# Where the conditioning slabs stand in the stream of weight slabs: behind every two or three weight slabs instead of behind each slab of a body's second half

## The reference

```
mods = silu(c) @ w_ada + b_ada                  # 9 vectors of 2048: shift, scale, gate of three stages
h = modulate(rms(x), sh1, sc1);  x += 0.5 * g1 * (silu(h@Wa) * (h@Wb)) @ w_ffn1_out
h = modulate(rms(x), sh2, sc2);  P = h @ w_in -> z, xBC, dt, u, gate_a, gate_b
A = ssd(conv(xBC), dt, z) @ w_a_proj;   B = glu(gelu(s5(u)) @ w_b_glu)
x += g2 * ((sigmoid(gate_a)*A + sigmoid(gate_b)*B) @ w_out)
h = modulate(rms(x), sh3, sc3);  x += 0.5 * g3 * swiglu(h, w_ffn2_in) @ w_ffn2_out;  rms(x)
```

## Time and profile before

| | |
|---|---|
| three runs | 2624.9 us median (2623.9 to 2632.23) |
| the profiled execution | 2625.14 us, span 2623.3 us |
| granted TensorE clock, mean over the span | 0.957 |
| busy share of the span | PE 94%, DVE 69%, ACT 39%, POOL 10% |

### The profile page before, as it was taken

How to read it: one execution, slowest core, us unless ns; L and a number is a source line. 1 busy time by engine, 2 the same in 40 slices (tenths; PEclk the granted TensorE clock), 3 DMA queues, 4 the chain that set the end, 5 groups by cost and what they waited for, 6 DMA issues and landing times. The chain is left out here.

```text
span 2623.3 us, 40243 instructions
## 1 busy us (share of the span) xinstructions
PE 2462.9 (94%) x16344; PEld 2272.9 (87%) x16344; DVE 1799.5 (69%) x2107; ACT 1015.1 (39%) x1074; POOL 271.7 (10%) x284
## 2 busy tenths in 40 slices
PE   6689999999999999899899979989999999999998
PEld 5668789978889988788799979989888899888998
DVE  4677877787786658899867776756876655444544
ACT  1043343334343344334434443333433444434433
POOL 0028823131421000000000000000000000000000
PEclk6599999999999989999999989999999999999999
DMA  8866786778787655454556656756687756555553
GB/s 293 319 225 241 266 294 241 272 276 309 260 310 247 234 181 193 146 179 159 176 178 208 209 177 225 242 200 231 222 307 243 246 177 201 191 183 180 194 170 108
DMA packets 296987, 584.54 MB, mean 223 GB/s; under 512 B 10324, under 2 KB 35412, under 8 KB 295316
## 3 DMA queue, kind: packets, MB, share of 16 engines
q1 hardware_dynamic: 292708, 560.32, 62.7%
q0 software_dynamic: 4144, 22.28, 2.4%
HBM read 569.98 MB, written 12.58 MB: 222 GB/s over the span
## 5 line engine op out<-in xcount | busy, mean ns | idle before, releaser
L883 DVE TENSOR_TENSOR wlo<-raw,whi 128x1024 fp32r<-128x1024 f32 x800 | 984.3, 1272 | 598.2 <-ACT whi L562 595.9
L562 ACT ACTIVATE whi<-raw 128x1024 fp32r<-128x1024 f32 x800 | 803.3, 1052 | 1330.0 <-PE gps L278 1182.0
L278 PE MATMUL gps<-whi,hs 128*128 128x512 f32 (+1 forms) x2816 | 873.0, 388 | 30.4 <-DVE wlo L883 19.9
L278 PE MATMUL gps<-hs,whi 128*128 128x256 f32 x3584 | 672.9, 290 | 59.4 <-DVE wlo L883 32.1
L278 PEld LDWEIGHTS gps<-whi,hs 128*128 128x128 f32 x2816 | 530.8, 189 | 138.7 <-DVE wlo L883 25.3
L278 PEld LDWEIGHTS gps<-hs,whi 128*128 128x128 f32 x3584 | 573.1, 197 | 71.8 <-DVE wlo L883 33.1
L278 PE MATMUL gps<-wlo,hs 128*128 128x512 f32 (+1 forms) x1408 | 543.9, 386 | 0.0
L278 PE MATMUL gps<-hs,wlo 128*128 128x256 f32 x1792 | 514.2, 287 | 0.0
L278 PE MATMUL gps<-ffs,whi 128*128 128x256 f32 x2752 | 498.5, 284 | 3.9 <-DVE wlo L883 3.7
L278 PEld LDWEIGHTS gps<-ffs,whi 128*128 128x128 f32 x2752 | 429.2, 192 | 5.4 <-DVE wlo L883 4.9
L901 DVE SCALAR_TENSOR_TENSOR acc<-raw,cact,acc 128x512 f32<-128x512 f32 x508 | 392.4, 772 | 16.3 <-DMA raw<-in_w_ada_dram 0.7
(11 more groups left out here) (233 smaller groups left out, 1341.9 us busy)
## 6 DMA issues: line engine op xcount, KB each, us to landing
raw<-in_w_ffn_in_dram SPq DMA_DIRECT2D x160, 1024.0 KB
raw<-in_w_ada_dram SPq DMA_DIRECT2D x144, 1024.0 KB
raw<-in_w_in_dram SPq DMA_DIRECT2D x80, 1024.0 KB
raw<-in_w_ffn_out_dram SPq DMA_DIRECT2D x56, 1024.0 KB
raw<-in_w_ffn_out_dram SPq DMA_DIRECT2D x40, 768.0 KB
raw<-in_w_a_proj_dram SPq DMA_DIRECT2D x16, 1024.0 KB
raw<-in_w_b_glu_dram SPq DMA_DIRECT2D x32, 512.0 KB
raw<-in_w_out_dram SPq DMA_DIRECT2D x16, 1024.0 KB
```

Of the source, the lines that this page charges most:

```text
L278: return pe.matmul(out, lhsT, rhs, start=start, stop=stop, skip_group_check=True)
L562: act.activation(whi[:, mpos % SPLIT, h, :], raw[:, pos % RING, h, :], ACT.Copy).then_inc(hi_ready, 1)
L883: ins = dve.tensor_tensor(wlo[:, mpos % SPLIT, h, :], raw[:, pos % RING, h, :], whi[:, mpos % SPLIT, h, :].bitcast(F32), ALU.subtract)
```

## The change

The order of a body's stream is written anew for all bodies with ada slabs except those flagged `fresh` (the first body behind a norm, and all four "in" bodies with ada slabs of the second feed-forward part). Nothing else is edited; DVE, PE, SP and ACT follow the stream.

```diff
-            if ada:
+            if ada and (fresh or n == 2):
                 self.stream += [("ada", 0, t) for t in range(4) if t * min(n, 4) // 4 == s]
+        if ada and not fresh and n > 2:
+            for t in range(4):
+                self.stream.insert((t + 1) * n // 2 + t, ("ada", 0, t))
...
-        first = [Phase("in", win, 0, NT, 1, "pair", "h", True, pair=FF),
+        first = [Phase("in", win, 0, NT, 1, "pair", "h", True, pair=FF, fresh=True),
...
-            Phase("in", win, 0, NT, 4, "pair", "h", True, pair=FF),
+            Phase("in", win, 0, NT, 4, "pair", "h", True, pair=FF, fresh=True),
...
-        + [("gemm", Phase("u", "w_in", OFF_U, NT, 1, "copy", "h", True, side="u")),
+        + [("gemm", Phase("u", "w_in", OFF_U, NT, 1, "copy", "h", True, side="u", fresh=True)),
```

More of the change, by code:

```diff
@@ L55, in __init__ @@
     def __init__(self, name, weight, col, k_tiles, bodies, evac, moving, ada=False, pair=0, row=0,
-                 narrow=False, start=0, gate=None, last=False, side=False, q0=0, norm=None):
+                 narrow=False, start=0, gate=None, last=False, side=False, q0=0, norm=None, fresh=False):
         self.name, self.weight, self.col, self.bodies, self.evac = name, weight, col, bodies, evac
```

## The result

The changed kernel takes 2679.72 us (median; 2678.76 to 2680.95) against 2626.16 us for the kernel before, measured beside it (2623.9 to 2632.23): a ratio of 1.0196, with an interval of 1.0183 to 1.021. It is 53.6 us slower. The profiled execution of the changed kernel took 2680.46 us with a span of 2678.7 us; the span before was 2623.3 us, so the two traces have 55.4 us between them to explain.

A forecast was written before the change was run, and what follows sets the result against it. PE, busy 94% of the span, was taken as the bound. New losses of 61.4 us less 19.8 given back, plus 2.1 in the gates, made +43.7 on 2625.14: 2669 us, range 2647 to 2684.

The forecast's parts named there:

- the first rival: Whole kernel: DVE and POOL take turns and the clock falls as worked out, 2669 us (2658 to 2680); chance 0.62.
- What the change can give back: PE's waits for `wlo` in the changed bodies, 194 to 784 us: at most 18.1 + 1.7 = 19.8 us.
- The head without POOL: Third slab of an "in" body: A0 and w02 on DVE would just fit, PE losing 0 to 0.3 us.
- POOL, played out as turns: "In" head: DVE and POOL alternate single operations behind L911, making the third slab 4.2 us late.
- The rule of the Trainium skill: "In" heads: each two-input DVE operation waits out a whole POOL operation; PE idles 5.5 us, kernel about 2679 us.
- The clock behind a head: Behind an "in" head's idle of 4.2 us the clock falls to the 1.2 GHz level, costing another 1.7 us.
- the first "in" behind "out": Head of that body: 6.5 us of room against 9.35, so 2.9 us lost and no fall of the clock.
- the two bodies beside POOL's constants: The two bodies before 286 us: 2.0 and 0.7 us new loss, +1.4 us net of the old loss.
- what I had at nothing outside the heads: `a_proj` and `w_out`: DVE is idle at the head for longer than A0 lasts, so 0.
- double heads: Two "in" heads with two pieces of POOL's: 13.6 us new loss, +9.3 us net of the old loss.
- The lower bound: "In" heads: A0 at 5.2 us and w02 at 3.23 lose 3.3 us each, clock stays up, 2649 us; chance 0.21.
- The faster rival: Whole kernel: bunched slabs are what costs and the heads fit, under about 1.2 us each, 2610 us; chance 0.03.

The follow-up runs named there:

- experiment 1: POOL's pieces from the third on cut from both orders: changed order 2624.54 us, ratio 0.9992 against the kernel before; old order 2611.83 us, ratio 0.9948.
- experiment 2: The changed kernel with each operation of POOL's pieces, from the third piece on, replaced by two memsets: 2622.38 us, ratio 0.9981 against the kernel before.
- experiment 3: POOL's pieces started later, in the middle of a body, in both orders: changed order 2655.59 us, ratio 1.0112 against the kernel before; old order 2670.1 us, 1.0176.
- experiment 4: The changed kernel with A0 behind w03, later ada slabs moved on in n = 4 bodies, old order for n = 6: 2635.22 us, ratio 1.0031 against the kernel before.
- experiment 6: POOL's pieces given out by a list of counts in both orders: old order 2614.58 us, ratio 0.9947 against the kernel before; changed order 2682.21 us, 1.0211.
- experiment 5: The new order only in `gate_a`, `gate_b`, `a_proj` and `w_out`, the first feed-forward part in the old order: 2629.16 us, ratio 1.0007 against the kernel before.

## Why the prediction was right, and where its sizes were off

The forecast was 2669 us with a range of 2647 to 2684; 2679.7 came out. The direction and the mechanism held, and the sum was nearly 12 us short (43.7 against 55.4 between the spans). At 2679.7 the time lies at the very edge of the first rival's own range, 2658 to 2680; part of what took it there, 3.8 us in `u`, has nothing to do with the change.

- **What the change can give back.** Right, and small: the old waits went in only a few places, and the spread gained 1.3 us in each "out" body of 20 tiles once the pieces were out of the way.
- **The head without POOL.** Predicted to lose 0 to 0.3 us; experiments 1 and 2 show 0.
- **POOL, played out as turns.** Predicted 4.2 us late; measured 3.79 and 3.69. Played out, the third slab's `wlo` was to be done 9.35 us behind L911; PE's start comes 9.06 us behind the end of L914 (361.59 - 352.53), each turn being a little shorter than assumed; and PE finished its second slab 5.27 us behind L914 (357.80), not 5.1. A0's first operation ran in 0.48 us, as assumed, since POOL came later than it. That it is reading SBUF that collides is shown by experiment 2, that the place is what costs by experiments 3, 4 and 6.
- **The rule of the Trainium skill.** The figure that the prediction worked out from "Who interferes with whom", 2679 us, is the one that came out, but not by its way: it had PE idle 5.5 us per head, and it idled 3.7 to 3.8. A whole operation of POOL's, 1.05 us, before each one of DVE's, 0.78, would be 1.83 us a step; the rows have 1.53. The rule itself holds in this trace: DVE's operations end 0.55 us behind POOL's. What was too much is the sum of two whole durations, since of the 0.75 us that such an operation takes alone only 0.55 comes after the wait. Experiment 2 agrees with the page on who takes part. The total agrees because other terms were larger, which is luck.
- **The clock behind a head.** Predicted 1.7 us. A single head lost 16.9 / 3 = 5.6 us, of which 3.7 is idle, which leaves 1.9. Experiment 6 has two bodies with the same idle of 3.68 us, one with no fall of the clock behind it (49.35 us long) and one with (50.93), so the clock itself costs 1.6.
- **First mis-sized term, the first "in" behind "out": +2.9 predicted, +6.2 measured.** The prediction gave the head 9.35 us and no fall of the clock. Here A0's first operation took a turn too, so that A0 and w02 took 10.3 us (530.62 to 540.9), PE idled 3.69 in place of 2.9, and the clock was at 0.50, the 1.2 GHz level, for 5.4 us or more:

```profile
530.47 0.15 DVE L914 TENSOR_TENSOR mods<-mps,pv 128x4 f32<-128x4 f32 x1
530.85 1.19 DVE L897 TENSOR_SCALAR acc<-raw,cact 128x512 f32<-128x512 f32 x1 [0.23 <-issue]
532.08 4.60 DVE L904 SCALAR_TENSOR_TENSOR acc<-raw,cact,acc 128x512 f32<-128x512 f32 x3
536.61 5.42 DVE L886 TENSOR_TENSOR wlo<-raw,whi 128x1024 fp32r<-128x1024 f32 x3
...
540.94 0.79 PE L281 MATMUL gps<-whi,hs 128*128 128x512 f32 x1 [3.69 <-DVE wlo L886]
```

- **Second, the two bodies beside POOL's constants: +1.4 predicted, +4.1 measured.** All of it is in the second of them; the first kept its length. POOL's smaller operations hold DVE up as well: A0 and w02 took 7.1 us (248.85 to 255.98) in place of 5.1, PE idled 2.19 and the clock was at 0.54 behind it, on average over 3.7 us. I had let only the larger operations count.
- **Third, what I had at nothing outside the heads.** `a_proj` and `w_out` lost 0.85 and 0.89 us, and experiment 5 shows them again (+0.82, +0.96) with the rest of the order unchanged, so they belong to the change. The traces say how. Ahead of `a_proj` PE idles for 16 us in both kernels and the clock is down. When the first body begins, it stays at 0.50 for 3.8 us more in the kernel before and for 5.7 us in the changed one, which costs 1 us:

```profile
1569.40:1573.20 3.80, 3.80 (x18) 3.80 (x19) 1.88 (x1) 0.00 (x0) 0.00 (x0) 0.50 0.00 0
```
```profile
1622.70:1628.40 5.70, 5.70 (x27) 5.70 (x28) 4.50 (x5) 0.00 (x0) 0.00 (x0) 0.50 0.01 3
```

  In `w_out` half of the loss is the same thing (PE works for 4.4 us at the lower level behind its idle of 7.04 us, before for 3.3), and the other half is where PE waits 0.17 us for `wlo` in the third slab.
- **Fourth, 3.8 us in `u`.** Its order is unchanged, PE idles for 3.8 and 3.9 us in its windows, and only the clock differs. The windows of the whole stage, in the kernel before, in the changed one, and in the old order of experiment 6:

```profile
926.60:1002.90 76.30, 72.50 (x524) 71.46 (x525) 51.48 (x110) 31.09 (x45) 2.30 (x3) 0.86 0.58 200
```
```profile
974.20:1054.20 80.00, 76.08 (x524) 75.17 (x524) 51.42 (x110) 31.02 (x44) 2.30 (x3) 0.81 0.55 191
```
```profile
916.00:995.90 79.90, 75.99 (x525) 75.07 (x525) 51.50 (x110) 31.16 (x45) 2.30 (x3) 0.82 0.56 191
```

The slower form shows under the old order as well, so this part isn't the order's doing; what decides between its forms was not found. Other kernels show lengths between (77.5 us in experiment 3), so that it is more than a switch between two. Without it the two traces are 51.6 us apart.
- **Terms that held:** double heads, the body at 286 us, narrow, "out" and the gates, each within 1.5 us.
- **The rivals.** The lower bound (heads of 3.3 us, no fall of the clock) was as near in the idle, 3.7 to 3.8, as the 4.2 of the turns; it failed on the clock, which fell behind every "in" head at which PE waited. The faster rival needed a head under about 1.2 us; with the pieces the heads cost 5.6, and even without them the new order was 12.7 us behind the old.

Open: what decides how long `u` runs at the lower clock, and what the "rest" of 1.3 us is made of.

## What to carry to other kernels

When work is moved behind a point where a semaphore is raised, look at who else is released there: here the same event that ended a chunk started POOL's piece, and moving 2.8 us of DVE's work next to it cost 5.6 us of PE's time at each head with one piece. An even spread is no gain in itself; what counts is the slot that each item lands in, how much slack DVE has there and who reads SBUF beside it. Placing the background engine's pieces into bodies with slack gained 13 us, and with the slabs of three bodies moved as well 17 us, by two small lists.

## What the hardware showed that I had not expected

**The clock doesn't follow the length of the idle alone.** In the old order of experiment 3 an idle of 1.87 us left it at 1.00 and one of 1.86 us brought it down:

```profile
553.37 0.50 PE L278 MATMUL gps<-whi,hs 128*128 128x512 f32 x1 [1.87 <-DVE wlo L891]
...
654.24 0.50 PE L278 MATMUL gps<-whi,hs 128*128 128x512 f32 x1 [1.86 <-DVE wlo L891]
```
```profile
553.40:556.80 3.40, 3.40 (x15) 2.83 (x16) 3.29 (x5) 0.14 (x1) 0.00 (x0) 1.00 1.01 319
...
654.30:657.70 3.40, 3.40 (x10) 2.68 (x11) 3.29 (x5) 0.12 (x1) 0.00 (x0) 0.61 1.07 317
```

At the other end, in the changed order of experiment 6, one of 3.68 us had no fall behind it (the window shows 1.00), though idles of that length elsewhere did:

```profile
644.11 0.50 PE L281 MATMUL gps<-whi,hs 128*128 128x512 f32 x1 [3.68 <-DVE wlo L886]
```
```profile
644.00:648.00 4.00, 3.89 (x17) 3.23 (x18) 4.00 (x4) 0.00 (x0) 1.89 (x2) 1.00 0.77 251
```

My reading of the earlier trace rows, 2.70 us stays and 3.46 us falls, was thus two draws from a scatter and no border. A stage can gain or lose some 4 us by it with its instructions and waits unchanged.

**An operation with one SBUF input takes a turn too:** L897 took 1.19 us at 530.85, where an operation of POOL's was running, and 0.48 us at 352.44, where POOL began behind it; the earlier trace rows had shown 1.28. It takes its turn with a memset as well, which reads nothing (experiment 2: 0.79 us at 785.36), and in that it differs from the operations with two inputs.

**Memsets on POOL cost DVE's operations with two inputs nothing:** at 0.53 us each, twelve of them beside A0 and `wlo`, these kept their undisturbed 2.33 and 2.35 us. Only A0's first operation lost, up to 0.3 us.
